# Weight sums with two rooms and a step of lag, a reordered store queue, and three rearranged places around a phase turn

## What is computed

```python
h = rms_norm(x, g_pre) * (1.0 + scale) + shift
x = x + gate * rms_norm(mixer(h), g_post)
# layer 0: mixer_ab
gq, gk, gv, gz, glr, rq, rk, rv, rz = split(h @ w_in_ab)
log_a = log_sigmoid(glr @ w_gate_up + b_gate) / 16       # gated linear attention
q_r, k_r = rotary(rq), rotary(rk)                         # retention
o, s = chunked_gated_linear_attn(q, k, v, lg, s0)
y = (norm(o) * silu(z)) @ w_out_ab
# layer 1: mixer_c
qkv, z, b_raw, a_raw = split(h @ w_in_c)                  # 3072 + 1024 + 16 columns
qkv = silu(causal conv of width 4 over qkv)
o, s = chunked_gated_delta(q, k, v, beta, log_g, s0)
y = (rms_norm(o) * silu(z)) @ w_out_c
```

## Time and profile before

| | us |
|---|---|
| median of 3 runs | 2617.94 |
| lowest and highest | 2615.05, 2620.39 |
| the profiled execution, its own time | 2615.59 |
| its span (first to last instruction) | 2613.8 |
| TensorE busy in the span | 2371.3 (91%) |
| VectorE, ScalarE, GpSimd busy | 1416.1, 968.0, 872.4 |
| mean granted TensorE clock | 0.957 of full speed |

### The profile page before, as it was taken

How to read it: one execution, slowest core, us unless ns; L and a number is a source line. 1 busy time by engine, 2 the same in 40 slices (tenths; PEclk the granted TensorE clock), 3 DMA queues, 4 the chain that set the end, 5 groups by cost and what they waited for, 6 DMA issues and landing times. The chain is left out here.

```text
span 2613.8 us, 58705 instructions
## 1 busy us (share of the span) xinstructions
PE 2371.3 (91%) x23067; PEld 1693.5 (65%) x23084; DVE 1416.1 (54%) x3034; ACT 968.0 (37%) x2726; POOL 872.4 (33%) x1092
## 2 busy tenths in 40 slices
PE   6989679679979999769999999996999999999997
PEld 2434234234555655258888888785888888888885
DVE  3332544534057785547777585555646555564655
ACT  3533244233311111324444343433444454444431
POOL 2541122121111111112322122115655656565652
PEclk9999899889989999879999999998999999999997
DMA  8543575572346444586676667556523222222213
GB/s 296 149 143 102 154 213 144 165 217 77 113 133 234 154 160 148 167 276 213 213 213 215 198 198 228 179 165 184 133 65 94 79 83 91 83 91 75 82 38 85
DMA packets 371527, 395.26 MB, mean 151 GB/s; under 512 B 39215, under 2 KB 262511, under 8 KB 371298
## 3 DMA queue, kind: packets, MB, share of 16 engines
q1 hardware_dynamic: 337186, 360.28, 43.8%
q10 hardware_dynamic: 34112, 31.71, 4.0%
HBM read 275.19 MB, written 116.72 MB: 150 GB/s over the span
## 5 line engine op out<-in xcount | busy, mean ns | idle before, releaser
L2728 DVE SCALAR_TENSOR_TENSOR inc_acc<-inc_ub,inc_taps,inc_acc 128x512 f32<-128x512 f32 x288 | 243.7, 846 | 9.2 <-ACT inc_acc L2571 2.4
L742 PE MATMUL inab_b<-inab_wt,keep 128*128 128x512 f16 x768 | 172.6, 387 | 30.9 <-ACT inab_vz L1064 20.0
L742 PE MATMUL inab_b<-inab_wt,raw_next 128*128 128x512 f16 x768 | 173.8, 390 | 21.1 <-ACT inab_vz L1064 21.1
L2507 POOL COPY inc_halo<-inc_ub 128x3 f32<-128x3 f32 x96 | 50.2, 525 | 363.6 <-DVE inc_ub L2716 224.1
L1344 PE MATMUL mixab_y<-keep,mixab_oT_hi 128*128 128x512 f16 x512 | 152.4, 379 | 7.1 <-DVE mixab_f_y L1424 5.4
L742 PEld LDWEIGHTS inab_b<-inab_wt,keep 128*128 128x128 bf16 (+1 forms) x768 | 75.9, 99 | 125.7 <-ACT inab_vz L1064 22.2
L742 PEld LDWEIGHTS inab_b<-inab_wt,raw_next 128*128 128x128 bf16 (+1 forms) x768 | 76.5, 100 | 117.3 <-ACT inab_vz L1064 23.3
L726 POOL TENSOR_TENSOR inab_a_out<-inab_stage,inab_a_out 128x384 f16<-128x384 f32 x64 | 61.3, 958 | 226.9 <-ACT inab_a_out L719 226.9
L712 DVE TENSOR_TENSOR inab_stage<-inab_m,inab_stage 128x512 f16<-128x512 f32 x64 | 44.1, 689 | 135.9 <-ACT inab_stage L722 135.9
L2837 PE MATMUL inc_b<-inc_room,keep 128*128 128x256 bf16 (+3 forms) x864 | 109.9, 279 | 2.4 <-DVE stage_next L2698 2.4
L3201 POOL TENSOR_TENSOR mixc_levels<-mixc_BT,raw_next 128x512 f32<-128x512 f32 (+1 forms) x82 | 110.3, 1376 | 1.5 <-DVE mixc_BT L3487 1.5
(11 more groups left out here) (619 smaller groups left out, 6363.4 us busy)
## 6 DMA issues: line engine op xcount, KB each, us to landing
keep<-tmp_w SPq DMA_DIRECT2D x336, 256.0 KB, 3.2
tmp_qkv<-inc_acc SPq DMA_DIRECT2D x96, 256.0 KB, 2.6
inab_stage<-in_w_in_c SPq DMA_DIRECT2D x128, 128.0 KB, 2.5
tmp_w<-inab_stage SPq DMA_DIRECT2D x64, 256.0 KB, 2.7
inab_stage<-in_w_in_ab ACTq DMA_DIRECT2D x24, 512.0 KB, 4.0
tmp_w<-inab_a_out SPq DMA_DIRECT2D x64, 192.0 KB, 2.1
stage_next<-in_w_ada ACTq DMA_DIRECT2D x6, 2048.0 KB, 14.9
raw_next<-tmp_qkv SPq DMA_DIRECT2D x8, 1536.0 KB, 6.8
```

What stands on the lines that cost most here:

```text
L742: last = nc.tensor.matmul(dst, lhs(a, k), rhs(b, k), start=(k == 0 and i == 0), stop=(k == KT - 1 and i == len(PASSES) - 1))
L2507: pool.tensor_copy(halo[:, g, :], ub[w % 2][side][:, BLK:]).then_inc(halo_saved[side], 1)
L2728: ins = dve.scalar_tensor_tensor(a_v, u_[:, i:i + BLK], taps[:, g, i:i + 1], a_v, ALU.mult, ALU.add)
```

## The change

- `PairWeights`: `a_out` has two rooms, and two semaphores for their stores; ScalarE does the upper part of the sums one step later (`sums_hi(n - 1)` ahead of `hi(n)`), VectorE the lower part two steps later (`sums_lo(n - 2)` ahead of `sums(n)`), and SyncE stores the sums of step n - 2 first thing in step n.
- The slots: 25 steps in each of blocks 1 and 2 and 14 in block 3, none at g = 10, 15 and 16. The output weights of layer 0 move to g = 23 to 30 of block 3.
- `outputs`: the x tile is fetched after the steps of g = 0 and 1; the store of `u` comes after the steps up to g = 9, the store of `r` after j = 3, and `u` and `r` are released at j = 9.
- Two small tables of the sample block come later, into the room of `a_out`.
- End of mixab: `scale_high` and `eye2` ahead of the last state add; GpSimd's three lower quarters and two of VectorE's are left out of the place; VectorE does three there (`lower_first`, `lower(2)`, `lower(1)`) and four (`first_left`) at the start of phase inc. One unit of ring weights is loaded instead of two; the second comes at the start of inc.
- Phase inc: x tile first; `zw` in eight DMAs behind items 1, 2, 5 and 8; the z items at places 5, 8, 14 and 15 of a block (before 3, 7, 11 and 15); the rest of the sample and the tails at the last item instead of behind it.

The sum of the arithmetic is the same. The core of the diff:

```diff
@@ PairWeights.next / sums / hi @@
         u, k = divmod(n, 4)
+        if n >= 2:
+            self.store_s(sp, n - 2)
         sp.wait_ge(self.a_lo, n + 1)
-        sp.dma_start(self.dst[u, 0:3, :, k].rearrange("m p e x -> p m e x"), self.a_out[:]).then_inc(self.a_stored, 16)
+        sp.dma_start(self.dst[u, 0:3, :, k].rearrange("m p e x -> p m e x"), self.a_out[n % 2]).then_inc(self.a_stored[n % 2], 16)
         if n + 2 < PAIR_STEPS:
             sp.wait_ge(self.s_done, n + 1)
             self.load(sp, n + 2)
-        if n >= 1:
-            self.store_s(sp, n - 1)
...
+        if n >= 2:
+            self.sums_lo(dve, n - 2)
         dve.wait_ge(self.raw_in[n % 2], 32 * (n // 2 + 1))
-        wait(dve, self.s_hi, n - 1)
         wait(dve, self.s_lo, n - 1)
...
+        if n >= 1:
+            self.sums_hi(act, n - 1)
         act.wait_ge(self.raw_in[n % 2], 32 * (n // 2 + 1))
-        wait(act, self.a_stored, 16 * n)
+        wait(act, self.a_stored[n % 2], 16 * (n // 2))
@@ slots @@
-    W7_TWICE = (16, 18, 20, 22, 24, 26, 28)
-    w7_slots = [g for g in order(BLK) for _ in range(2 if g in W7_TWICE else 1) if not 5 <= g < 7]
+    W7_SLOTS = (0, 1, 2, 3, 4, 7, 8, 9, *range(17, 31))
+    W7_TWICE = (20, 24, 28)
+    w7_slots = [g for g in W7_SLOTS for _ in range(2 if g in W7_TWICE else 1)]
+    W7_BLOCK, W7_LAST = len(w7_slots), 23
...
+    ROWS_AT = {W7_LAST + i: i for i in range(KT)}
@@ outputs @@
-            next_x(0)
-            w7_next(b, 0, 1, 2, 3, 4, 7, 8)
...
+            w7_next(b, 0, 1)
+            next_x(0)
+            w7_next(b, 2, 3, 4, 7, 8)
+            next_x(1)
+            w7_next(b, 9)
+            store_u()
             for j in range(4 * tiles):
...
                 w7_next(b, 15 + j)
...
+                if j == 1:
+                    next_x(2)
+                if j == 3:
+                    store_r()
+                if j == 6:
                     next_x(3)
+                if j == 9:
+                    sp.wait_ge(out, 80 * (b + 1))
+                    sp.sem_inc(u_free, 1)
+                    sp.sem_inc(r_free, 1)
@@ mixab, vector and sync @@
         for p in range(PAIRS):
+            if p == PAIRS - 1:
+                early.scale_high(dve)
+                dve.tensor_copy(eye2...).then_inc(eye_ready, 1)
             dve.wait_ge(kv_done, nt + p + 1)
...
-        early.scale_high(dve)
         dve.wait_ge(cond.mm, 6)
         early.differences(dve)
-        early.lower(dve)
-        dve.wait_ge(o_done, nt + 1)
-        dve.tensor_copy(eye2...).then_inc(eye_ready, 1)
+        early.lower_first(dve)
         fin.mean_sample(dve, nt)
+        early.lower(dve, 2)
         dve.wait_ge(gate_in, 48)
         fin.gated_sample(dve, nt, 0, 16 * (nt // 2 + 2))
+        early.lower(dve, 1)
@@ inc @@
-    ORDER = (0, 1, 2, (0, 0), 3, 4, 5, (0, 1), 6, 7, 8, (1, 0), 9, 10, 11, (1, 1))
+    ORDER = (0, 1, 2, 3, 4, (0, 0), 5, 6, (0, 1), 7, 8, 9, 10, 11, (1, 0), (1, 1))
...
+        for dst, src, hi in io["first_left"]:
+            dve.tensor_tensor(dst, src, hi, ALU.subtract).then_inc(first_lo, 1)
...
+        FIRST_LEFT = {2: 1, 7: 2, 4: 3, 3: 4}
...
+            if n == 0 and i in FIRST_LEFT:
+                pe.wait_ge(first_lo, FIRST_LEFT[i])
```

More of the change, by code:

```diff
@@ L661, in __init__ @@
         self.src, self.dst, self.raw, self.s_out, self.banks = src, dst, raw, s_out, banks
-        self.a_out = ph.sb("a_out", [P, 3, 2, P], F16)
+        self.room = ph.sb("a_out", [P, 6 * P])
+        self.a_out = [self.room[:, i * 3 * P:(i + 1) * 3 * P].bitcast(F16).rearrange("p (m e x) -> p m e x", m=3, e=2) for i in range(2)]
         s = ph.sem
@@ L968, in _ @@
         sp.wait_ge(pre_in, 64)
[L969 to L971 removed]
+        w7.stored(sp, w7.s_stored)
         for i in range(4):
@@ L1006, in _ @@
                     w7.lo(pool, step)
-        prep.rstd(pool, nt, 0, NS)
-        prep.split_lo(pool, nt, 0, NS, prep.at(nb))
-        for u in range(KT):
-            rows_out.lo(pool, u)
+        for g in order(BLK):
+            if g == SQUARE[0]:
+                prep.rstd(pool, nt, 0, NS)
+            if g == HI_S:
+                prep.split_lo(pool, nt, 0, NS, prep.at(nb))
+            for step in w7_at(nb - 1, g):
+                w7.lo(pool, step)
+            if g in ROWS_AT:
+                rows_out.lo(pool, ROWS_AT[g])
     @block.scalar
@@ L1108, in _ @@
             groups(b, BLK, [(4 * b + 4 + tc, P) for tc in range(4)])
-        w7.room_free(act)
-        rows_out.load(act, 0)
-        groups(nb - 1, BLK, [(nt, NS)], rows_at={**dict(zip(range(16, 30, 2), range(7))), 30: 7})
+        groups(nb - 1, BLK, [(nt, NS)], rows_at=ROWS_AT)
         groups(nb, NS, [])
@@ L1606, in phase_mix_ab @@
                   tv["ident"], io["modT"][:, 1], cond.modT_ready, operands(io),
-                  [stage_next[:, i * D:(i + 1) * D].rearrange("p (k n) -> p k n", k=4) for i in range(4)])
+                  [stage_next[:, i * D:(i + 1) * D].rearrange("p (k n) -> p k n", k=4) for i in (2, 3, 0, 1)])
+    io["first_left"] = early.left()
     block = ph.block()
```

178 lines of the change are left out of this document (102 added, 76 removed).

## The result

| | before | changed |
|---|---|---|
| median of 4 runs, us | 2616.49 | 2475.17 |
| lowest and highest | 2612.84, 2620.39 | 2471.05, 2477.84 |
| span of the profiled execution | 2613.8 | 2469.2 |
| TensorE busy, share of the span | 91% | 95% |
| mean granted TensorE clock | 0.957 | 0.978 |

The ratio is 0.9458, with a 95% interval of 0.9438 to 0.9478: 141 us less. I had said 2499, with a range from 2484 to 2540. The sign and most of the places were right, the size was not: the result lies 9 us under the low end.

A forecast was written before the change was run, and what follows sets the result against it. Blocks 1 and 2 of inab were taken to wait on the order of things, a ring of engine waits, not on work. Terms -97.7 - 9.9 - 9.5 + 2.5 - 3.5 = -118.1 from 2615.6 gave 2497.5, median about 2499; range 2484 to 2540.

The forecast's parts named there:

- Blocks 1 to 3: Phase inab: stalls of blocks 1 and 2 go, 44.7 and 48.9 us less, and block 3 4.1 less; sum -97.7.
- 1.5 us a block for leftovers: Blocks 1 and 2 of inab: allowance for remaining waits, added to a clean 131.5 to give 133 us.
- 25 steps are 93 us, under the block's 133: Blocks 1 and 2 of inab: at 3.7 us a step with latency, the weight-sum steps fit into the block.
- Rival 4: inab: two rooms only move ScalarE's wait to the sums, only moved steps count; 2542 us, chance 0.16 shared with another rival.
- The turn: End of mixab to inc's first product: short differences, `eye2` wait gone, gated add ends at 1110.9 instead of 1120.8; -9.9 us.
- the -4.4 that long ones would have given: End of mixab: the term if VectorE's two differences stayed at 4.96 and 3.03 us despite GpSimd doing nothing there.
- Start of inc: First products of inc: TensorE's 7.0 us refill wait and 2.5 of clock go; -9.5 us, bounds 0 and -10.
- Inside and end of inc: Five convolution items in a row cost +2.5 us (bounds 0, +10); z items last save 3.5 (bounds 0, -5).
- another 1.3 for the delayed third sum: End of inc: the sample convolution on VectorE delays the last third sum by about 1.3 us.
- where I had added 2.3: Whole kernel: the median of the runs was taken to lie 2.3 us above the profiled execution.
- the sum of the good bounds: Whole kernel: all terms at their best, -102.7 - 10 - 10 - 5 - 0, gives 2490 us; range has 6 us margin below.
- one ring: inab blocks 1 and 2: SyncE waits for VectorE's rotary, `a_out`'s store is late, ScalarE stands with full banks, TensorE stops.

## Why the prediction was wrong, and where it was right

**Block 0: the step that failed.** My sum starts with "Blocks 1 to 3"; block 0 has no term, so I took it as unchanged. The diff reorders SyncE's queue in every block, and the trace of before had both the 15.05 us of ScalarE and the 9.27 us of TensorE in block 0. I looked at the queue only for the sake of the steps, and block 0 has none. Measured: -11.8, of which 9.3 are the wait, about 1.5 the lower clock behind it (0.90 granted from 166 to 180), and 1.0 lies ahead of it. With that term the forecast would have been 2487 and the low end of the range 2472, with the measured 2475 inside. It is 12 of the 24 us.

**Blocks 1 to 3: size nearly right, reason not.** The terms were 44.7, 48.9 and 4.1, and it was 46.7, 50.8 and 6.2: the "1.5 us a block for leftovers" were not there, since TensorE is never kept waiting. But "25 steps are 93 us, under the block's 133" was no argument. By the same line 32 steps are 118 us and fit as well, and they do not fit: 148 and 154 us with every other part of the change in place. What I left out is that SyncE stands some 28 us a block in front of VectorE whatever the number, a wait whose other face, 14.8 us in front of the rotary, stood in the earlier trace rows. 28 + 3.7 x 25 is 120, under 131; for 32 it is 146. That the number of steps decides is shown; this line for it fits block 1 in four runs and is otherwise read from the waits. The change needs its 7 steps fewer a block, and I had booked them as a detail beside the two rooms. Rival 4 came nearer to what happened than I allowed. Its mechanism, that the two rooms move ScalarE's wait from the store of `a_out` to the sums, is in the trace, but at 25 steps the moved wait costs TensorE nothing. Its price for the moved steps, 7 x 3.7 us a block or 52 us in two, was near too: moving them alone took away 57.

**The turn: right.** -9.9 forecast and measured. GpSimd beside the differences, 5.5 of it, is shown as a cause by a run; the rest, the lower quarters and `eye2` taken out of the way, is read from the timelines. My sum for it went by the short differences and not by the -4.4 that long ones would have given.

**Start of inc: right.** -9.5 forecast, -9.6 measured, and the gate-weight loads as its cause are shown, at 13.3 us in the changed kernel.

**Inside and end of inc: too careful.** +2.5 and -3.5 forecast, -1.1 and -4.9 measured. My forecast counted from the end of the last product, before the eight transposes: counted so, it is -0.2 inside, and 11.8 to 6.1, -5.7, at the end, which is beyond my bound of -5. VectorE keeps up with five convolution items in a row: TensorE waits for its sums in this stretch for 3.5 us at convolution items and 0.6 at z items, where it was 3.1 and 2.7. I had taken +2.5 for this, so the sign of that term was wrong. At the end 6.1 us are left behind the last product, where I had 7 and another 1.3 for the delayed third sum. No run tests these two places by themselves.

**The rest.** Some 3 us of the profiled difference came from mixab by chance. The profiled execution of the changed kernel, 2471.05 us by its own time, lies 4.1 us below its median, where I had added 2.3; that is why 144.6 us between the spans are 141 between the medians. The errors of the other terms all had one sign, and the low end had only 6 us of margin under the sum of the good bounds; it should have held a place that I had not looked at. Two slips in my sums are small: the turn's own terms give 1110.8 and not 1110.9, and 44.7 + 48.9 less two times 26 is 42, where rival 4 adds 43. No rival's time came true.

## What to carry to other kernels

When a queue is reordered, list every stage that runs through that code, also those without the work that the change is about, and look in each for an engine that waits on that queue. A queue that serves a chain of steps has a budget: the number of steps times the time of one, plus all the time in which the queue stands in front of other engines. Compare that sum with the stage, and not the steps' time alone. Here it fits one block within 3 us and is too low for the next, which also takes over what was left undone. And where several parts of a change loosen one ring, taking each away by itself says little: here three parts cost 8 to 12 us each in blocks 1 to 3 when removed alone, 31 in sum, and 48 when removed together.

## What I had not expected of the hardware

What VectorE and GpSimd cost each other also lengthens GpSimd's short operations. In the changed kernel the 128x1 power that the gated add waits for took 1.45 us, beside a lower quarter on VectorE:

```profile
988.79 1.45 POOL L1453 TENSOR_TENSOR mixab_f_rs<-mixab_f_ms,mixab_f_mhalf 128x1 f32<-128x1 f32 x1 [18.13 <-DVE mixab_f_ms L1448]
```

```profile
988.63 1.21 DVE L1579 TENSOR_TENSOR stage_next<-stage_next 128x1024 f16<-128x1024 f32 x1
```

In the kernel before it took 0.54 us with nothing of the kind beside it. So up to 0.9 us of the turn (an estimate, 1.45 less 0.54) are still to be had if that quarter stood behind the power's end; this was not run.

The same lies behind part of the 16 us by which VectorE's busy time has grown in the three blocks of inab. The first of the four sums of a step, L711, takes 301 ns in the median but over 400 ns in 13 of 64 steps, where before it was 2 of 64. The longest took 2134 ns, from 238.12 on: a GpSimd operation ran from 237.98 to 240.10, and the sum ended 0.15 us after it. TensorE is not kept waiting by any of this here.
